# A two-layer decoder trunk on eight cores: the SSM scan held at every fourth position instead of every second

## What is computed

```python
def ssm_branch(u, h0_re, h0_im, a_re, a_im, log_step, b_re, b_im, c_re, c_im, d_skip, w_glu, b_glu):
    ab_re, ab_im, bb_re, bb_im = ssm_discretise(a_re, a_im, log_step, b_re, b_im)
    bu_re = jnp.einsum('gnc,btgc->btgn', bb_re, uf)          # 32 groups x 16 channels, 64 states
    bu_im = jnp.einsum('gnc,btgc->btgn', bb_im, uf)
    # h_t = A h_{t-1} + B u_t, all complex, A diagonal
    p_re, p_im, h_re, h_im = lax.associative_scan(
        complex_affine_combine, (a_r, a_i, bu_re, bu_im), axis=1)
    y = (jnp.einsum('gcn,btgn->btgc', c_re, h_re)
         - jnp.einsum('gcn,btgn->btgc', c_im, h_im) + d_skip * uf)
    z = jax.nn.gelu(y)
    out = z * jax.nn.sigmoid(z @ w_glu + b_glu)
```

## Time and profile before

| | us |
|---|---|
| median of 3 runs | 4232.08 |
| lowest, highest | 4217.65, 4252.25 |
| the profiled execution | 4279.33 |
| span of its slowest core | 4278.3 |
| spans of all cores | 4205.7 to 4278.3 |
| SSM of layer 0: preparation to 144.2, loop to about 604 | 604 |
| SSM of layer 1: preparation from 2193, loop to 2776 | 583 |

### The profile page before, as it was taken

One profiled execution on the slowest core, in us unless ns is written; L12 is line 12 of the kernel. 1 busy time (PEld: TensorE's weight loads), 2 busy tenths in 40 slices (PEclk: granted clock), 3 DMA queues, 4 the chain that ended last, 5 costly groups with the idle time before them and its releaser, 6 DMA issues.

```text
span 4278.3 us, 49429 instructions; the slowest of 8 cores (4205.7 to 4278.3 us)
## 1 busy us (share of the span) xinstructions
PE 2536.8 (59%) x16520; PEld 1381.3 (32%) x16520; DVE 2450.2 (57%) x4645; ACT 1480.0 (35%) x2089; POOL 273.8 (6%) x224
## 2 busy tenths in 40 slices
PE   2344434499953976776613344354799449857773
PEld 0344333144421332332302334342344113323322
DVE  5888864334344753565257888843444448446633
ACT  1233334122243642553222332242222446335522
POOL 0000000000000111001100000000100001100111
PEclk6665665688875998898756666656899769979986
DMA  5000010433314788547920000003433256974697
GB/s 101 21 1 1 1 23 6 27 32 32 70 59 98 96 80 92 99 45 71 127 78 30 1 1 1 12 12 21 44 32 70 79 124 67 100 125 45 60 82 117
DMA packets 573146, 233.72 MB, mean 55 GB/s; under 512 B 515808, under 2 KB 535008, under 8 KB 572640
## 3 DMA queue, kind: packets, MB, share of 16 engines
q0 software_dynamic: 490640, 137.90, 32.3%
q1 hardware_dynamic: 82256, 92.67, 7.6%
HBM read 329.39 MB, written 39.05 MB: 86 GB/s over the span
## 4 chain that ended last, share of the span: by engine, by line
DVE 34%; PE 26%; issue 19%; DMA 11%; ACT 9%; DVEq 1%; ACTq 0%; SPq 0%; POOL 0%; POOLq 0%
PE psa L131 26%; DVE arena L142 21%; DVE arena L151 9%; ACT arena L139 7%; DMA arena<-w_dn 4%; DVE arena L157 2%; DMA res<-arena 1%; ACT L139 1%; DMA arena<-w_in 1%; DMA arena<-w_up 1%; DMA arena<-res 1%; DVEq L228 1%; ACT arena L155 1%; DMA o_pool_s<-arena 1%; DMA arena<-cpad 1%
## 5 line engine op out<-in xcount | busy, mean ns | idle before, releaser
L131 PE MATMUL psa<-arena 128*128 128x512 bf16 (+3 forms) x16520 | 2536.8, 326 | 1705.1 <-DVE arena L142 794.7
L131 PEld LDWEIGHTS psa<-arena 128*128 128x128 bf16 (+1 forms) x16520 | 1381.3, 115 | 2860.3 <-issue 2256.0
L142 DVE TENSOR_TENSOR arena<-arena 128x512 f32<-128x512 f32 (+10 forms) x2420 | 1286.2, 568 | 610.3 <-ACT arena L139 229.5
L139 ACT ACTIVATE arena<-arena 128x1024 f32<-128x1024 f32 (+6 forms) x636 | 580.5, 924 | 575.9 <-DVE arena L157 303.9
L151 DVE SCALAR_TENSOR_TENSOR arena<-arena 128x1024 f32<-128x1024 f32 (+5 forms) x562 | 543.5, 970 | 266.5 <-ACT arena L139 228.2
L155 ACT COPY arena<-psa 128x512 f32<-128x512 f32 (+1 forms) x682 | 353.3, 538 | 307.0 <-PE psa L131 281.6
L139 ACT ACTIVATE arena<-psa,arena 128x128 f32<-128x128 f32 (+3 forms) x416 | 221.0, 540 | 490.6 <-PE psa L131 460.1
L139 ACT ACT_TABLE_LOAD x148 | 189.9, 1283 | 551.0 <-DVE arena L151 306.0
L151 DVE SCALAR_TENSOR_TENSOR arena<-arena,psa 128x128 f32<-128x128 f32 (+1 forms) x296 | 144.0, 487 | 401.1 <-PE psa L131 335.7
L142 DVE TENSOR_TENSOR arena<-psa,arena 128x512 f32<-128x512 f32 (+2 forms) x274 | 159.6, 587 | 330.7 <-PE psa L131 172.8
L155 ACT CAST arena<-arena 128x512 bf16<-128x512 f32 (+2 forms) x73 | 133.5, 1828 | 525.7 <-DVE arena L151 482.3
(11 more groups left out here) (21 smaller groups left out, 120.0 us busy)
## 6 DMA issues: line engine op xcount, KB each, us to landing
arena<-w_dn POOLq DMA_DIRECT2D x80, 704.0 KB, 11.4
arena<-w_up POOLq DMA_DIRECT2D x88, 512.0 KB, 7.0
res<-arena SPq DMA_DIRECT2D x12, 2048.0 KB, 7.4
arena<-res SPq DMA_DIRECT2D x12, 2048.0 KB, 13.7
arena<-w_in POOLq DMA_DIRECT2D x16, 768.0 KB, 9.7
arena<-bpad SPq DMA_DIRECT2D x16, 512.0 KB, 6.2
arena<-xT SPq DMA_DIRECT2D x4, 2048.0 KB, 9.1
yT<-arena SPq DMA_DIRECT2D x4, 2048.0 KB, 7.5
```

Source lines behind the costliest of these rows:

```text
L131: self.op('pe', lambda e: e.matmul(out, lhsT, rhs, start=start, stop=stop), r, w)
L139: self.op('act', lambda e: e.activation(out, in_, func, **kw), r, w)
L142: self.op(eng, lambda e: e.tensor_tensor(out, a, b, op), r, w)
```

## The change

The state is held at every fourth position: LS = 4 phases of NJ = 32 columns in a block of the prompt, SJ = 2 states in a sampled sequence of 8. For this the preparation makes A to the powers 2, 3, 4 and k times A to the powers 1, 2, 3 (cmul), four input operands lbs (before two), three output operands lgs (before one) and three direct terms kms (before one). The tables of the rotation use four times the angle, with 32 columns. In the loop stage_BU adds four products of 32 columns for each state group and part, the scans have 256 columns, and stage_CY makes four phases, of which the phase e below the last adds e+1 direct terms.

```diff
+        LS = 4
+        NJ = 128 // LS
+        SJ = 8 // LS
...
-        lb1 = P.alloc("lhsT_B1", [128, 2, 16, 128], BF16)
-        lb0 = P.alloc("lhsT_B0", [128, 2, 16, 128], BF16)
+        lbs = [P.alloc(f"lhsT_B{e}", [128, 2, 16, 128], BF16) for e in range(LS)]
...
+        def cmul(xr_, xk, xi_, xik, yr_, yk, yi_, yik, slot):
...
+            P.tt(ta, xr_, yr_, ALU.mult, [xk, yk], [kta])
+            P.tt(tb, xi_, yi_, ALU.mult, [xik, yik], [ktb])
+            P.tt(orr, ta, tb, ALU.subtract, [kta, ktb], [okr])
+            P.tt(ta, xr_, yi_, ALU.mult, [xk, yik], [kta])
+            P.tt(tb, xi_, yr_, ALU.mult, [xik, yk], [ktb])
+            P.tt(oii, ta, tb, ALU.add, [kta, ktb], [oki])
...
+        for m in range(2, LS + 1):
+            apow[m] = cmul(*apow[m - 1], abr, kabr, abi, kabi, slot)
+            slot += 2
+        for m in range(1, LS):
+            kpow[m] = cmul(*kpow[m - 1], abr, kabr, abi, kabi, slot)
+            slot += 2
...
-            for (ks_r, kk_r, ks_i, kk_i, lbx) in ((kr, kkr, ki_, kki, lb1), (akr, kakr, aki, kaki, lb0)):
+            for e_ in range(LS):
+                (ks_r, kk_r, ks_i, kk_i) = kpow[LS - 1 - e_]
+                lbx = lbs[e_]
...
+            for e_ in range(LS - 1):
+                (pr_, pk_, pi_, pik_) = apow[e_ + 1]
+                lgx = lgs[e_]
...
+                P.tt(t53, cre3, arb, ALU.mult, [cre.k(), pk_], [t5.k()])
+                P.tt(t63, cim3, aib, ALU.mult, [cim.k(), pik_], [t6.k()])
...
+            for d_ in range(LS - 1):
+                (fr_, fk_, fi_, fik_) = kpow[d_]
...
+                P.tt(t53, b2r3, krb, ALU.mult, [b2r.k(), fk_], [t5.k()])
+                P.tt(t63, b2i3, kib, ALU.mult, [b2i.k(), fik_], [t6.k()])
+                P.tt(xrb, t53, t63, ALU.subtract, [t5.k(), t6.k()], [xr.k()])
...
+                    P.cp(kms[d_][:, cc, :], pk[:, 0:128], [pk.k()], [kms[d_].k(cc)], eng='act')
...
-                    P.mm(pbx[:, gl, :], lb0[:, ri, gp, :], ub[:, gp // 4, 0, :], True, False, [lb0.k(), ub.k()], [pbx.k()])
-                    P.mm(pbx[:, gl, :], lb1[:, ri, gp, :], ub[:, gp // 4, 1, :], False, True, [lb1.k(), ub.k()], [pbx.k()])
+                    for e_ in range(LS):
+                        P.mm(pbx[:, gl, :], lbs[e_][:, ri, gp, :], ub[:, gp // 4, e_, :], e_ == 0, e_ == LS - 1,
+                             [lbs[e_].k(), ub.k()], [pbx.k()])
...
-            P.op('dve', lambda e, dk=dk: e.tensor_tensor_scan(sc[6][:, 0:512], dk, sc[4][:, 0:512], 0.0, ALU.mult, ALU.add),
+            P.op('dve', lambda e, dk=dk: e.tensor_tensor_scan(sc[6][:, 0:NE], dk, sc[4][:, 0:NE], 0.0, ALU.mult, ALU.add),
...
-                for eo in range(2):
-                    out = py[:, cc * 128 + eo * 64:cc * 128 + eo * 64 + 64]
+                for e_ in range(LS):
+                    out = py[:, cc * 128 + e_ * NJ:cc * 128 + (e_ + 1) * NJ]
+                    last = (e_ == LS - 1)
+                    nmm = 8 if last else 8 + e_ + 1
...
+                    if not last:
+                        for e2 in range(e_ + 1):
+                            P.mm(out, kms[e_ - e2][:, cc, :], ub[:, cc, e2, :], False, idx == nmm - 1, [kms[e_ - e2].k(), ub.k()], [py.k()])
+                            idx += 1
```

More of the change, by code:

```diff
@@ L481, in _build @@
         wglu = P.alloc("wglu", [128, 4, 512], BF16)
-        lb1 = P.alloc("lhsT_B1", [128, 2, 16, 128], BF16)
-        lb0 = P.alloc("lhsT_B0", [128, 2, 16, 128], BF16)
+        lbs = [P.alloc(f"lhsT_B{e}", [128, 2, 16, 128], BF16) for e in range(LS)]
         lc = P.alloc("lhsT_C", [128, 2, 16, 128], BF16)
[L485 to L491, removed]
+        lgs = [P.alloc(f"lhsT_G{e}", [128, 2, 16, 128], BF16) for e in range(LS - 1)]
+        kms = [P.alloc(f"km{d}", [128, 4, 128], BF16) for d in range(LS - 1)]
+        Ec = P.alloc("Ec", [128, 16, NJ], F32)
+        Es = P.alloc("Es", [128, 16, NJ], F32)
+        DkP = P.alloc("DkP", [128, 16, NJ], F32)
+        DkS = P.alloc("DkS", [128, 16, NJ], F32)
+        pw = P.alloc("pw", [128, 48, 16], F32)
         pwi = P.alloc("pwi", [128, 16], I32)
@@ L607, in _build @@
-            for cq in range(2):
-                cc = 2 * hfs + cq
-                pk = bank(2 + cq)
-                idx = 0
-                for gq in range(4):
-                    gp = cc * 4 + gq
-                    gl = gp - H0
-                    for (xb_, ri) in ((xrb, 0), (xib, 1)):
-                        P.mm(pk[:, 0:128], xb_[:, gl, :], lc[:, ri, gp, :], idx == 0, idx == 7,
-                             [xr.k(), xi.k(), lc.k()], [pk.k()])
-                        idx += 1
-                P.cp(k0m[:, cc, :], pk[:, 0:128], [pk.k()], [k0m.k(cc)], eng='act')
@@ L637, in _build @@
-        ufl = [P.alloc(f"uf{i}", [128, 4, 2, 64], F32) for i in range(2)]
-        brl = [P.alloc(f"br{i}", [128, 8, 64], F32) for i in range(2)]
-        bil = [P.alloc(f"bi{i}", [128, 8, 64], F32) for i in range(2)]
-        hb = P.alloc("hb", [128, 2, 8, 80], BF16)
+        pbr = P.psum_buf("pbr", 512, NE, [128, 8, NJ])
+        pbi = P.psum_buf("pbi", 1536, NE, [128, 8, NJ])
+        ubl = [P.alloc(f"ub{i}", [128, 4, LS, NJ], BF16) for i in range(2)]
+        ufl = [P.alloc(f"uf{i}", [128, 4, LS, NJ], F32) for i in range(2)]
@@ L641, in _build @@
+        brl = [P.alloc(f"br{i}", [128, 8, NJ], F32) for i in range(2)]
+        bil = [P.alloc(f"bi{i}", [128, 8, NJ], F32) for i in range(2)]
+        hb = P.alloc("hb", [128, 2, 8, HBW], BF16)
         zf = P.alloc("zf", [128, 4, 128], F32)
```

152 lines of the change are left out of this document (76 added, 76 removed).

## The result

| | before | after |
|---|---|---|
| median, 26 runs each, taken in turn | 4293.14 us | 4272.46 us |
| lowest | 4217.65 | 4247.24 |
| ratio after to before, 95% interval | | 1.0067 [1.0047, 1.0087] |
| profiled execution | 4279.33 | 4255.92 |

In some executions the cores of one die run slower, whatever the kernel; the medians hold such runs and the ratios do not, which is why the ratio counts here: the change costs 0.67%, about 28 us (20 to 37). Forecast were 8 us. The sign is right, and the size is some 20 us off, with 8 us outside the interval. The sign says little by itself: the prediction put 0.65 on no difference that could be told from none, and counted 1% as such.

The account below looks back on a forecast made before the run. The prediction took DVE to bound the loop, with the preparation wholly on its path. Loops -255 us and preparation +263 make +8, on the median of 4232.08 giving 4240 us; the range leaving out 2 in 10 was 4195 to 4300.

Parts of the forecast that it names:

- The bound: SSM part: DVE is the long pole of the loop, and every step of the preparation goes through it.
- The preparation: Ahead of each layer's loop: more rounds 140+120 us, powers of A 12, narrower tables -9; 263 us more in all.
- what would show it: Signs listed for the forecast, among them a preparation of 185 to 195 us where it was 127 and 123.5.
- Scans and narrow products: DVE in the loop, 512 to 256 columns: scans 1218 to 691 ns, products 686 to 425; 8.4 us less per block.
- Rival 3: Loop, DVE: halved operations shrink by less because of dependences; a tenth of 8.4 us lost, 28 us, 4268; chance 0.13.
- The narrow matmuls: stage_BU and stage_CY on PE: a 32-column matmul with its weight load takes 27 ns at the lower clock.
- Rival 1: stage_BU and stage_CY: load and matmul stay at 53 ns, block about 21.3 us, total 4291; chance 0.22.
- The step that failed: tailB: Loop, DVE: tailB waits 0.5 us for the sigmoids until 7.92, then ends at 8.5 us.
- The walk through the block: One loop block timed step by step from the first stage_ROT: 27.25 us falls to 19.7, 7.55 less.
- -255 forecast for the loops: Both layers' loops: 34 blocks, each 7.5 us shorter, 255 us less.
- the +8: Whole kernel: net of 255 us less in the loops and 263 us more in the preparation.
- Rival 2: PE keeps its full clock in the lhsT_B rounds (28 us less) and the GLU (17 less): 4195; chance 0.10.

Follow-up runs that it names:

- the loop alone: The changed kernel with its preparation cut to the rounds of the kernel before, SSM values wrong: 4018.06 us.
- the preparation alone: The kernel before, its loop unchanged, with the preparation given the work of the changed one: 4527.59 us.
- the plain store: The changed kernel with tailB's bf16 product stored side by side, positions in wrong order: ratio to the kernel before 1.0027 [0.9999, 1.0055].

## Why the prediction was right in direction and short in size

**The bound: right.** DVE is the busiest engine of the new block too (15.87 of 20.20 us, PE 11.47), and the preparation lies in full ahead of the loop: the loop alone left the loops at 333 us, the preparation alone added 129 and 130 us to the preparations and hardly anything to the loops (451.8 and 450.4, after 450.3 and 450.2).

**The preparation: right.** Forecast +251 in the rounds and tables and +12 for the powers; the windows show 125.8 + 122.9 = 248.7, and +5.8 ahead of layer 0 and about as much ahead of layer 1, 260 in all where 263 was forecast. A round of lhsT_B lasts 17.5 us and one of lhsT_G 7.6 (106.08 to 113.67 below), the 16 matmuls of km hide:

```profile
98.39 6.26 DVE L142 TENSOR_TENSOR arena<-arena 128x1024 f32<-128x1024 f32 x5 [5.99 <-DMA arena<-cpad]
104.75 1.23 DVE L151 SCALAR_TENSOR_TENSOR arena<-arena 128x1024 bf16<-128x1024 f32 x1
106.08 6.16 DVE L142 TENSOR_TENSOR arena<-arena 128x1024 f32<-128x1024 f32 x5
...
113.67 6.16 DVE L142 TENSOR_TENSOR arena<-arena 128x1024 f32<-128x1024 f32 x5
```

One sentence on what would show it gave 185 to 195 us for the preparation. That contradicts the sum beside it, which asks for about 250, and it was the sentence that was wrong: 252.8 and 246.4.

**Scans and narrow products: right.** 691 ns forecast, 685 and 666 measured; 425 and 419 for the products. Rival 3 falls.

**The narrow matmuls: right.** 27 ns forecast at the lower clock, 27.1 measured (76 in 2.06 us), 25 at the full one. Rival 1 needed 40 and falls. The Trainium skill's figure of about 60 cycles for up to 64 columns ("TensorE: Matmul & The Clock Gate", "Back-to-back issue gap") would be 50 ns were it cycles of the gated clock; the trace disagrees with that reading, and agrees with the 25 ns at 2.4 GHz that the same page gives for 32 columns.

**The step that failed: tailB.** The walk through the block let tailB pass from 7.92 to 8.5 us, 0.6 us, which is the price of an operation that stays as it is. This one does not: the change widens its output pattern, so that the bf16 values are stored 8 bytes apart and not 4.

```diff
-            yav = ya[:, :, c0:c0 + 128].rearrange("p c (j e) -> p c e j", e=2)
+            yav = ya[:, :, c0:c0 + 128].rearrange("p c (j e) -> p c e j", e=LS)
```

The prediction's list of what the change adds in the loop has no such term. Measured from 434.26, the walk held up to there: the scans end at 4.7 (4.75 forecast), the sigmoids at 7.92 (7.92), and tailB starts at 8.02. Its record is 1.32 us long where it was 0.73, and the next operation starts 1.1 us behind it and not 0.6. Everything that follows is late by this half microsecond: the carry cast at 11.17 (10.6), the last stage_CY at 16.28 (15.75), the skip additions at 18.58 (18.07), the block's end at 20.20 (19.7). 34 blocks make 17 us of it, and the plain store gave back 17.6.

**What is left.** -255 forecast for the loops, some -241 measured (7.09 a block by the window of layer 0); the +8 becomes +19 by the windows of this core, +23 by the means over all cores, +28 (20 to 37) by the ratio. The 5 us between the last two are within what one execution differs from another: the mean span of the eight cores is 4231.7 to 4252.7 us in the executions of after that the ratio counts, and 4201.5 to 4217.0 in those of before that were taken beside the experiments. The traced execution of before, with 4215.4, lies near the top of its range, and that of after, with 4238.4, below the middle of its own.

**Rival 2** named two stretches in which PE would keep its full clock, and it did so in neither: the granted clock of the preparation was 0.58 and 0.57, and that of the GLU matmuls 0.50 (the window at 437.19), so the sigmoids came no earlier. Only stage_BU of the next block ran at the full clock (1.00 in the window at 446.17).

## What to carry to other kernels

Holding a state more sparsely moves work from a loop into its preparation, and is worth what the preparation costs: here the loop saved 7.1 us in each of 34 blocks and the preparations paid 8 more rounds of 17.5 us and 16 of 7.6. Of each 17.5 us, 7.8 were waits, most of which a second pair of buffers removed. Price the preparation by its waits and not by its work alone, and pipeline it before judging the change: as written it lost 0.7%, with pipelined rounds and a reordered block it gains 2.5% (0.975 [0.9724, 0.9776]), and 1.7% by estimate over the kernel before with its own rounds pipelined. And where a diff changes a factor of interleaving, follow it into every access pattern: an operation of the same size and count can take nearly double (0.73 and 1.32 us here).

## What was not expected of the hardware

- A bf16 store 8 bytes apart takes 1296 ns for 512 columns on DVE and 1326 on ACT, against 727 and 762 at 4 bytes and 698 and 618 side by side; fp32 stores and reads 8 bytes apart are free (693, 692).
- POOL and DVE take turns on tensor products from SBUF: 16.5 us for what takes 9.5 and 7.5 apart, and 1.88 us for a DVE operation of 16 columns beside one of POOL.
- 32-column matmuls with a weight load each keep 27 ns at 1.2 GHz and gain almost nothing at 2.4 GHz (25 ns), so the clock hardly matters for them here.
